# Eight transposed blocks of mLSTM V, drained later in the projection loop of a one-core Trainium2 kernel

## The reference

```python
h = rmsnorm(x, norm_pre) * (1 + scale) + shift
u = h @ w_in
q_a, k_a, v_a, z_a, q_m, k_m, v_m, o_m, z_m, i_m, f_m, g_a, g_m = split_in(u)
att = attend(q_a, k_rows, v_rows, lam)          # prompt: own keys; sample: paged cache
att = rmsnorm(att, attn_head_norm) * (1 - lam_init)
y_a = (att * silu(z_a)) @ w_br_a
hm, C1, n1, m1 = mlstm(qm, km, vm, ig, lf, C0, n0, m0)
y_m = (sigmoid(o_m) * rmsnorm(hm) * silu(z_m)) @ w_br_m
y = (sigmoid(g_a) * y_a + sigmoid(g_m) * y_m) @ w_out
out = x + gate * rmsnorm(y, norm_post)
```

## Time and profile before

| what | value |
|---|---|
| time, median of three runs | 2077.53 us (2071.15 to 2080.35) |
| the profiled execution's own time | 2070.42 us |
| its span, first to last instruction | 2068.9 us |
| TensorE busy | 2012.0 us, 97% of the span |
| TensorE weight loads busy | 1709.6 us, 83% |
| VectorE busy | 762.5 us, 37% |
| ScalarE busy | 641.0 us, 31% |
| GpSimd busy | 181.2 us, 9% |
| mean granted clock of TensorE | 0.989 of full speed |
| DMA | 238.39 MB, mean 115 GB/s |

### The profile page before, as it was taken

One profiled execution on the slowest core, in us unless ns is written; L12 is line 12 of the kernel. 1 busy time (PEld: TensorE's weight loads), 2 busy tenths in 40 slices (PEclk: granted clock), 3 DMA queues, 4 the chain that ended last, 5 costly groups with the idle time before them and its releaser, 6 DMA issues.

```text
span 2068.9 us, 32041 instructions
## 1 busy us (share of the span) xinstructions
PE 2012.0 (97%) x12650; PEld 1709.6 (83%) x12650; DVE 762.5 (37%) x1659; ACT 641.0 (31%) x1152; POOL 181.2 (9%) x285
## 2 busy tenths in 40 slices
PE   5999999999999999999999999999999999999997
PEld 3779999988888878889999977777777777777775
DVE  4445334266622233443445322322232232352224
ACT  3312222245544444343233222222212212332221
POOL 2000102000020100122230000000000000110002
PEclk8999999999999999999999999999999999999999
DMA  9972332231244521223343333333343343453223
GB/s 300 324 267 74 99 102 78 72 98 52 65 147 131 168 69 54 54 72 102 90 131 82 82 111 97 107 120 107 98 129 100 109 116 111 131 198 91 77 77 117
DMA packets 144241, 238.39 MB, mean 115 GB/s; under 512 B 14369, under 2 KB 80033, under 8 KB 142377
## 3 DMA queue, kind: packets, MB, share of 16 engines
q1 hardware_dynamic: 124704, 177.24, 28.3%
q0 software_dynamic: 17168, 59.17, 8.8%
q10 hardware_dynamic: 2242, 0.19, 0.1%
HBM read 218.84 MB, written 17.71 MB: 114 GB/s over the span
## 4 chain that ended last, share of the span: by engine, by line
PE 74%; DVE 2%; ACT 1%; POOL 1%; issue 1%; DMA 0%; ACTq 0%; DVEq 0%; POOLq 0%
PE gemm L509 56%; PE bank_s L509 9%; PE bank_a L509 3%; PE bank_o L509 3%; PE bank_s L746 1%; DVE g_m L1979 1%; PE bank_s L920 0%; ACT L1126 0%; PE bank_a L692 0%; DVE y_tok L2055 0%; POOL hm_sq L2240 0%; POOL hm_sq L2241 0%; ACT w_hi L1126 0%; ACT sq_att L1126 0%; POOL rinv L2306 0%
## 5 line engine op out<-in xcount | busy, mean ns | idle before, releaser
L1486 DVE TENSOR_TENSOR w_lo<-w_raw,w_hi 128x512 fp32r<-128x512 f32 x512 | 357.1, 699 | 865.3 <-ACT w_hi L1126 864.6
L509 PE MATMUL gemm<-h_hi,w_hi 128*128 128x288 f32 (+1 forms) x2560 | 666.2, 326 | 3.4 <-DVE z_act L1874 1.7
L1126 ACT ACTIVATE w_hi<-w_raw 128x512 fp32r<-128x512 f32 x512 | 322.2, 630 | 1098.1 <-PE bank_s L509 613.6
L509 PE MATMUL gemm<-h_hi,w_lo 128*128 128x288 f32 (+1 forms) x2560 | 642.2, 316 | 0.0
L509 PE MATMUL gemm<-h_lo,w_hi 128*128 128x288 f32 (+1 forms) x2560 | 641.6, 316 | 0.0
L509 PEld LDWEIGHTS gemm<-h_hi,w_hi 128*128 128x128 f32 x2560 | 428.2, 190 | 86.0 <-issue 52.5
L509 PEld LDWEIGHTS gemm<-h_hi,w_lo 128*128 128x128 f32 x2560 | 429.0, 190 | 20.5
L509 PEld LDWEIGHTS gemm<-h_lo,w_hi 128*128 128x128 f32 x2560 | 428.9, 190 | 19.7
L509 PE MATMUL gemm<-w_hi,y_all 128*128 128x512 f32 x512 | 159.6, 393 | 0.4 <-DVE g_m L1979 0.4
L509 PEld LDWEIGHTS gemm<-w_hi,y_all 128*128 128x128 f32 x512 | 95.3, 188 | 27.9 <-issue 3.9
L509 PE MATMUL gemm<-w_lo,y_all 128*128 128x512 f32 x256 | 100.0, 391 | 0.0
(11 more groups left out here) (440 smaller groups left out, 1809.8 us busy)
## 6 DMA issues: line engine op xcount, KB each, us to landing
w_raw<-in_w_in SPq DMA_DIRECT2D x384, 256.0 KB, 2.8
ada_in<-in_w_ada SPq DMA_DIRECT2D x32, 1024.0 KB, 8.8
ada_g<-in_w_ada POOLq DMA_DIRECT2D x32, 512.0 KB, 4.3
w_raw<-in_w_out SPq DMA_DIRECT2D x64, 256.0 KB, 2.4
k_page<-in_cache_k POOLq DMA_DIRECT2D x16, 512.0 KB, 5.5
v_page<-in_cache_v POOLq DMA_DIRECT2D x16, 512.0 KB, 4.7
w_raw<-in_w_br_a SPq DMA_DIRECT2D x32, 256.0 KB, 2.4
w_raw<-in_w_br_m SPq DMA_DIRECT2D x32, 256.0 KB, 2.5
```

Source lines behind the costliest of these rows:

```text
L509: return nc.tensor.matmul(out, lhsT, rhs, start=start, stop=stop, skip_group_check=True)
L1126: return nc.scalar.activation(out, in_, func, **kw)
L1486: V.tensor_tensor(w_lo[:, slot], w_raw[:, slot], w_hi[:, slot], ALU.subtract).then_inc(lo_ready, 1)
```

## The change

In pairs 17 to 19 `to_tokens` and `tok_v` move from granules 0 and 1 to granules 2 and 6 (the third and the seventh). Before the transposes TensorE waits there for the second half of the keys to have left bank_s, which `scores_s` of the same step waited for already. The wait for `tok_done` goes from behind the transposes to ahead of `norm_sum`, one granule later. In pair 20 the transposes stay in granules 0 and 1, and the wait moves behind `weights_s` in the first and behind `values_s` in the second.

```diff
@@ TensorE @@
-                if 17 <= p <= 20 and g < 2:
-                    n = 16 + 2 * (p - 17) + g
-
-                    if c % 4 == 0:
-                        pe.wait_ge(an_r, 2 * (c // 4) - 1)
-                    elif c < 32:
-                        pe.wait_ge(kt_sb, 2 * (c // 4) + 1)
-                    else:
-                        pe.wait_ge(bc_sb, 1)
-                    to_tokens(v_stage[:, g, :], (bank_free[g], V0 + p), (tok_done, n), tok_ps)
-                    pe.wait_ge(tok_done, n + 1)
+                if 17 <= p <= 19 and g in (2, 6):
+                    n = 16 + 2 * (p - 17) + g // 4
+                    pe.wait_ge(kt_sb, 2 * (c // 4) + 2)
+                    to_tokens(v_stage[:, g // 4, :], (bank_free[g // 4], V0 + p), (tok_done, n), tok_ps)
+                if p == 20 and g < 2:
+                    pe.wait_ge(*((bc_sb, 1) if g else (an_r, 2 * NB - 1)))
+                    to_tokens(v_stage[:, g, :], (bank_free[g], V0 + p), (tok_done, 22 + g), tok_ps)
                 if c % 4 == 0 and 1 <= c // 4 <= 8:
                     weights_s(c // 4 - 1)
                 if c % 4 == 1 and 1 <= c // 4 <= 8:
                     values_s(c // 4 - 1)
+                if p == 20 and g < 2:
+                    pe.wait_ge(tok_done, 23 + g)
...
                     if c % 4 == 3:
                         pe.wait_ge(kt_sb, 2 * b + 2)
+                        if p >= 17:
+                            pe.wait_ge(tok_done, 17 + 2 * (p - 17) + g // 4)
                         norm_sum(b, bank_s[:, 0, :])
@@ VectorE @@
-                if 17 <= p <= 20 and g in (0, 1) and d != 1:
-                    tok_v(v_mls[:, 0:NT, :], v_mls[0:NS, NT, :], 16 + 2 * (p - 17) + g, 2 * (p - 17) + g)
+                if 17 <= p <= 19 and g in (2, 6):
+                    tok_v(v_mls[:, 0:NT, :], v_mls[0:NS, NT, :], 16 + 2 * (p - 17) + g // 4, 2 * (p - 17) + g // 4)
+                if d == 0:
+                    tok_v(v_mls[:, 0:NT, :], v_mls[0:NS, NT, :], 22, 6)
```

## The result

The changed kernel takes 2058.26 us, median of five runs (2055.48 to 2064.87), against 2077.53 us before. The ratio is 0.9922 with a 95% interval of 0.9894 to 0.995: faster by 10 to 22 us, which is 0.5 to 1.1%. Measured again in two further sets, each beside runs of the kernel before, the ratio was 0.9936 (0.9922 to 0.995) and 0.9929 (0.9912 to 0.9946). The forecast was 2065.5 us in a range of 2057 to 2073, and 12.0 us of gain.

The account below looks back on a forecast made before the run. TensorE, busy for 97% of the span, was taken to bound the kernel. Gains of 10.35 + 1.62 = 11.97 us, rounded to 12.0, off the median of 2077.53 us gave 2065.5 us, range 2057 to 2073 us.

Parts of the forecast that it names:

- Pairs 17 to 19, 10.35 us: In these three pairs, 3.45 us each of TensorE's waiting and pipeline refilling around two V blocks would go: 10.35 us.
- Nothing is late next: In pairs 17 to 19, the bias comes 0.27 us late, 0.57 stays spare before `norm_sum`; cost zero, at most 3.8 us.
- Pair 20, 1.62 us: In pair 20, granule 0 gains 0.65 us and granule 1 gains 0.97 us, 1.62 us together.
- Sum and forecast: Whole kernel: 10.35 + 1.62 = 11.97 us gained, 2065.5 us forecast from the median; chance 0.55.
- More, by the clock: Rival: the clock's fall behind pair 20's wait goes too, 1.72 us more, gain 13.7 us, 2063.8 us; chance 0.22.
- The refill: In pair 20's granule 0, `mls_bcast` pays 0.27 us behind the wait; weight loads pulled ahead would gain 0.27 more.
- The change doesn't free TensorE: Rival: pairs 17 to 19 keep most of their 44.17 us, held by ScalarE's root and key copy; 2075.9 us; chance 0.07.
- Slower, by the clock: Rival: transposes in the third and seventh granule bring clock falls, 1.72 us each; 1.8 us slower, 2079.3 us; chance 0.06.
- The sign that I had named for being wrong: A clock under 1.00 between 560 and 750 us, or TensorE waiting on `sq_att`, `k_t` or k_page in pairs 17 to 19.

## Why the prediction was right

- *Pairs 17 to 19, 10.35 us.* Right. Measured 10.56 us, in every trace of the changed kernel. Halves of 20.36 us were foreseen and 20.33 measured. That a half without transposes served as the model for one with them is what made this term safe. The experiments show that it takes both edits: the place takes off the part of the wait that hangs on ScalarE's root, the later wait covers the copies.
- *Nothing is late next.* Right in kind, with a smaller delay than worked out: the bias starts 0.13 us later against the scores (0.20 behind them instead of 0.07), not 0.27, because the two small attention copies held VectorE for 0.20 us and not the 0.29 that I had given them, and the split in front of them for 0.60 from its start to the next and not 0.67. To spare were 0.72 us, not 0.57. The doubled copies showed that beyond it each block pays the excess and a refill.
- *Pair 20, 1.62 us.* Right in kind and somewhat small where the clock stays: 1.88 us. The step that was off is the refill that `mls_bcast` was to pay, 0.27 us: by the chain it takes 1.12 us behind the wait and 1.05 without one, so granule 0 gains 0.92 - 0.07 = 0.85 us and not 0.65. In granule 1 the 0.97 us of idling left out what `values_s` paid behind it, 1.92 instead of 1.85 us, so 1.04 went. The two are 1.89. In the profiled execution only 18.23 - 17.88 = 0.35 us came of it, since the fall cost 3.05 us there and 1.52 in the trace of before.
- *Sum and forecast.* 11.97 us against 12.4 without falls, and 11.8 to 13.6 by runs of like clock. The plain means differ by 2075.9 - 2060.7 = 15.2 us and the first two medians by 19.3. The term that was mis-sized is the clock's, which I put at zero in the forecast and at 1.72 us, one fall in pair 20, in the rival *More, by the clock*. From pair 17's start to L813 the three traces of before take 150.8, 155.3 and 152.2 us, the four of the changed kernel 139.9, 136.8, 139.9 and 138.3: means of 152.8 and 138.7, 14.1 apart, so 1.7 us more than the 12.4 that came without falls. The remaining 1 us of the means and the rest of the 19.3 lie behind pair 20, where the traces of before scatter by 6 us and those of the changed kernel by 12. That the first median came as far as 7.2 us under the forecast is in part chance: the two further sets gave 2062.1 and 2061.4, 3.4 and 4.1 under it.
- *The refill.* By the rule of the Trainium skill ("TensorE: Matmul & The Clock Gate", Engine queue depth in its first table), that weight loads may be pulled ahead of running matmuls, held over a wait, the pair would have gained 0.27 more. It did gain 0.26 more, but not so: in none of these waits does a weight load start before the wait ends. The traces show two kinds of work. `weights_s`, `values_t` and `norm_sum` have their first weight load 0.13 or 0.14 us ahead of the matmul when nothing is waited for (639.62 and 639.76, 630.76 and 630.89, 635.59 and 635.72 in the trace of before), which agrees with the page, and within 0.04 us of it behind a wait; they hold 0.27, 0.22 and 0.24 us more behind one (0.92 for 0.65, 0.44 for 0.22, 1.10 for 0.86). `mls_bcast`, `values_s` and `keys_t` start load and matmul within 0.01 us of each other either way and hold 0.07 more (1.12 for 1.05, 1.92 for 1.85, 1.09 for 1.02). So what a wait costs on top of its idling hangs on what stands behind it, and the wait ahead of `mls_bcast` was cheaper than I had put it.
- *The change doesn't free TensorE.* It does: `keys_t` follows `weights_s` at once (616.72), and no wait on `k_t` came up.
- *More, by the clock.* The case had to be likelier than I made it. I weighed one trace of before, in which three long waits of pairs 17 to 19 had brought no fall, and read from it that pair 20's fall was chance. The 14 traces show a fall in pair 20 in 10 of 11 in which TensorE waited 1.5 or 2.2 us there, and in none of 3 in which it waited 0.3. By the length of pair 20 a fall cost about 1.5 us in five of the ten and about 3 in the other five. A wait of that length is not enough by itself, though: behind the waits of pairs 17 to 19 it is 1 in 9 before, and 1 in 3 with the wait alone moved. The Trainium skill's rule ("TensorE: Matmul & The Clock Gate", Part 1: The HAM clock gate), that idling brings the clock down and sustained work brings it back, agrees with pair 20 in these numbers, and does not say why the others mostly kept their clock.
- *Slower, by the clock.* It did not come: in none of the four traces of the changed kernel was there a fall in pairs 17 to 19. The sign that I had named for being wrong, a clock under 1.00 between 560 and 750 us, did show in the profiled execution (0.66 in 740 to 750). It is pair 20's fall, which the shorter pairs moved ahead of 750; the sign was set too wide to tell the two apart.

## What to carry to other kernels

Where an in-order engine waits for a copy out of a shared buffer, look both at what the copying engine is doing when the buffer is filled and at what the waiting engine could do before it writes the buffer again; the first decides where the producer should stand, the second where the wait should. A stretch of the same loop without the work is the best model of the loop after the work is hidden. Take more than one trace before calling a fall of the clock chance, and a granule behind the same work as the measure of what a fall cost.

## What was not expected of the hardware

A wait of TensorE of 1.5 to 2.2 us in a place with small matmuls around it came with a fall from 2.4 to 1.2 GHz (granted clock 0.50) in 10 of 11 traces, which cost 1.5 or 3 us on the spot; cut to 0.3 us, the wait came with none in 3. That the whole kernel gains as much is not shown, since the falls behind 900 us differ by more from run to run. Most of the scatter of the kernel before (2066.31 to 2081.27 us over its runs) goes with the mean granted clock, about 2 us for each 0.001 of it ((2077.9 - 2068.6) / 5, between 0.984 and 0.989), so runs are better compared at like clock. A wait also costs TensorE more than its idle time: 0.2 to 0.3 us where the next weight load would have run ahead of its matmul, 0.07 where it would not.
